# Differential attention: the next product in its last units, its casts spread over two engines, and two small VectorE instructions merged or replaced

## Chip, cores and metric

The kernel runs on one core of a Trainium2 chip. The metric is the device time of one execution in microseconds (us). Before the change three runs took 2040.03, 2040.24 and 2040.45 us; the median is 2040.24.

## The reference

Two transformer blocks over 512 tokens of width 1024, all in fp32. The first block is a sliding-window attention with retention and a convolved feed-forward; the second is a half feed-forward, a token mix and another half feed-forward. The change is in the token mix, whose first part is the differential attention (8 heads, each with two components of 64 and values of 128):

```
s = einsum('bqhcd,bkhcd->bhcqk', qb, k) * scale          # c: the two components
s = where(kpos <= qpos, s, NEG_INF)
p = softmax(s, axis=-1)
a = p[:, :, 0] - lam * p[:, :, 1]
o = einsum('bhqk,bkhe->bqhe', a, v)
y_da = rmsnorm(o, head_gain) * (1 - lam_init)
```

Behind it come the second attention (NSA: compressed, selected and windowed parts with gates), two projections, and the output product. The columns of `w_in` that give the second attention's values and gate logits are the product that the change moves.

## The kernel before

Every fp32 product is made of three passes over operands split in a high part (a cast to fp32r) and a low part (the difference): high x high, high x low, low x high (`three`, L666). Weights are streamed: chunks of 128 x 1024 are loaded by SyncE into six slots (L475 to L478), ScalarE casts the high part (`split`, L1255) and VectorE makes the low part (`split`, L1768). A chunk's slot is free when TensorE has counted it used (`w_used`). Each engine has its own program, in order; the engines meet only in semaphores.

A **unit** t of the differential attention is one head t//4 and one block t%4 of 128 query rows, so its width is 128, 256, 384 or 512 keys; there are 32. The parts of a unit are spread over the engines, two units ahead of each other:

- TensorE, step t (L853): values of unit t-2 (`values`, L825), scores of unit t+2 for both components in two PSUM banks (`scores`, L801), transpose of unit t (`turn`, L816), and one eighth of a chunk of the product `nsf` (`nsf_steps`).
- ScalarE, step t (L1450): output of unit t-2 (`da_out`), cast of the transposed probabilities (`high`), sometimes casts of the operands of a later head (`high_parts`), then the exponentials of unit t+2 (`exps`), which need the row maxima.
- VectorE, step t (L1994): `combine` (L1970: a reciprocal, the factor `gg` as a SCALAR_TENSOR_TENSOR of one element per partition, and the difference of the two components in place), `low` (the low part of the transposed probabilities), `maxima` of unit t+2 (L1963, one reduction for each component), and at the units of `LOW_AT` the low part of a weight chunk.
- GpSimd: the low parts of a head's queries and keys (`qk_low`, L537) and values (`v_low`, L553), each instruction behind a drain.

A head's operands are staged so: ScalarE casts Q and K for both components in four casts in a row (`high_parts(..., 0)`, L1467) at units with t%4 == 3 (for the head after the next), and V in one cast at t%4 == 1 (for the next head); GpSimd makes the low parts as they come (semaphore `st_hi`, counted in `st_lo`); SyncE copies the K cast to the other half of the partitions (`TWIN_AT`, L452). Scores of a head wait for `st_lo` and `k_twin` (L805), values for the fifth count of the head (L829).

Behind the attention TensorE makes the product `nst` (L1035): three chunks, four tiles each of 128 rows x 304 columns in banks 0 to 3, nine products a tile in the first two chunks and six in the last. ScalarE and VectorE meanwhile norm the attention's output: squares (L1626), their sums (L2211), a root (L1629), the multiplication by its reciprocal (L2219), then the rotated keys (`keys_out`, L2225), and the high and low parts of the product (L1635, L2239). Then `rope_q` and the compression follow (L1104).

Of the kernel before, what the change touches and what calls it, by code (L numbers as in the profile page):

```python
# [14 lines left out]
P = 128  # L15
# [8 lines left out]
LEAD = 5  # L24
# [75 lines left out]
def program(nc, t, out, stop=None):  # L100
# [9 lines left out]
    with ExitStack() as ctx:  # L110
# [170 lines left out]
        ps = [ctx.enter_context(nc.psum_tensor(f"ps{b}", [P, 512], F32)) for b in range(8)]  # L281
# [44 lines left out]
        k_twin = sem("k_twin")  # L326
        mx_done = sem("mx_done")
# [51 lines left out]
        LOW_AT = (6, 10, 14, 22, 30)  # L379
# [45 lines left out]
        def _(sp):  # L425
# [14 lines left out]
            def swaps(m):  # L440
# [51 lines left out]
        def _(pl):  # L492
# [43 lines left out]
            if on("da"):  # L536
                def qk_low(it, head):  # L537

                    u = head % 2
                    q = qkd[:, span(it, 2, head, 1), :].rearrange("p a n -> p (a n)")  # L540
                    for m in range(2):
                        own, other = slice(HD * m, HD * m + HD), slice(HD * (1 - m), HD * (1 - m) + HD)
                        pool.drain()
                        pl.wait_ge(st_hi, 5 * head + m + 1)
                        pool.tensor_tensor(Qst[other, u, m, :], q[own, :], Qst[own, u, m, :], ALU.subtract).then_inc(st_lo, 1)
                    k = qkd[:, span(it, 2, 8 + head, 1), :].rearrange("p a n -> p (a n)")
                    for m in range(2):
                        own = slice(HD * m, HD * m + HD)
                        pool.drain()
                        pl.wait_ge(st_hi, 5 * head + m + 3)  # L550
                        pool.tensor_tensor(Kl[own, u, m, :], k[own, :], Kh[own, u, m, :], ALU.subtract).then_inc(st_lo, 1)

                def v_low(it, head):  # L553
                    u = head % 2
                    pool.drain()
                    pl.wait_ge(st_hi, 5 * head + 5)
# [103 lines left out]
        def _(pe):  # L660
# [140 lines left out]
            def scores(t):  # L801
# [3 lines left out]
                if i == 0:  # L805
                    pe.wait_ge(st_lo, 5 * (t // 4) + 4)
# [18 lines left out]
            def values(t):  # L825
# [3 lines left out]
                if t % 4 == 0:  # L829
                    pe.wait_ge(st_lo, 5 * (t // 4) + 5)  # L830
# [17 lines left out]

            def attention():
# [3 lines left out]
                for t in range(TOTAL):  # L853
# [181 lines left out]
            if on("nst"):  # L1035
                for c in range(3):
                    s = weights(CHUNK0["nst"] + c)
                    for tt in range(TT):
                        q = slice(tt * P, (tt + 1) * P)
                        if c == 0:  # L1040
                            bank_free("nst", tt)
                        for j, k in enumerate(range(c * VG_K, min(c * VG_K + VG_K, KT))):
                            n = slice(j * VG_W, (j + 1) * VG_W)
                            last = three(ps[tt][:, 0:VG_W], HTh[:, k, q], HTl[:, k, q], Wh[:, s, n], Wl[:, s, n], k == 0, k == KT - 1)
                    last.then_inc(w_used, 1)
# [208 lines left out]
        def _(ac):  # L1254
# [183 lines left out]
            def nsf_out(c):  # L1438
                chunk_done("nsf", c)
                if c >= 2:  # L1440
                    ac.wait_ge(st_lo, 5 * (4, 7)[c - 2] + 2)
# [3 lines left out]
            def attention():  # L1445
                exps(0)
                high_parts(0, 0, 1)
                exps(1)
                high_parts(0, 1, 0)
                for t in range(TOTAL):  # L1450
# [16 lines left out]
            def high_parts(it, head, which):  # L1467

                u = head % 2
                if which == 0:  # L1470
                    q = qkd[:, span(it, 2, head, 1), :].rearrange("p a n -> p (a n)")
                    for m in range(2):
                        own = slice(HD * m, HD * m + HD)
                        scalar.copy(Qst[own, u, m, :], q[own, :]).then_inc(st_hi, 1)
                    k = qkd[:, span(it, 2, 8 + head, 1), :].rearrange("p a n -> p (a n)")
                    for m in range(2):
                        own = slice(HD * m, HD * m + HD)
                        scalar.copy(Kh[own, u, m, :], k[own, :]).then_inc(st_hi, 1)
                else:
                    if head == 0:  # L1480
                        ac.wait_ge(free[6], FREED["da"][6])
                    scalar.copy(Vst[:, u, 0, :].rearrange("p (t n) -> p t n", t=TT), vd[:, :, span(it, 2 * P, head * P, P)]).then_inc(st_hi, 1)
# [128 lines left out]
            if on("vda"):  # L1611
                for c in range(7):
                    split(CHUNK0["vda"] + c + LEAD)
                    if c == 3 and on("da"):
                        ac.wait_ge(roped, 24)
                        high_parts(0, 0, 0)
# [5 lines left out]
            if on("nsf"):  # L1622
# [5 lines left out]
                ac.wait_ge(da_ss, 2)  # L1628
                scalar.activation(hsd[:], hss[:], ACT.Sqrt, scale=1.0 / P, bias=eps[:]).then_inc(da_sd, 1)  # L1629
            if on("nst"):  # L1630
                split(CHUNK0["nst"] + 1 + LEAD)
# [4 lines left out]
                for tt in range(TT):  # L1636
                    scalar.activation(gates[:, tt, :], ps[tt][:, 2 * P:VG_W], ACT.Sigmoid).then_inc(vs_hi, 1)
# [944 lines left out]
```

## Time and profile before

| | us |
|---|---|
| median of 3 runs | 2040.24 |
| profiled execution, own time | 2040.7 |
| its span in the trace | 2038.9 |
| TensorE busy | 1990.8 (98%) |
| VectorE busy | 1052.6 (52%) |
| ScalarE busy | 818.6 (40%) |
| GpSimd busy | 275.5 (14%) |
| mean granted TensorE clock | 0.993 |

The profile is one execution on the chip. Times in the trace are counted from the span's start; the differential attention lies between 1107 and 1220 us. PE is TensorE's matmul queue and PEld its weight loads, DVE is VectorE, ACT is ScalarE, POOL is GpSimd, SP is SyncE. A granted clock of 1.00 is 2.4 GHz and 0.50 is 1.2 GHz. "<-" in a bracket names what ended a wait.

### The profile page before, as it was taken

The numbers are of one execution on the slowest core, as the hardware profiler recorded it, in microseconds if no ns is written. First come the engines' busy times: TensorE is split into PE (matmuls) and PEld (weight loads), VectorE is DVE, ScalarE is ACT, GpSimd is POOL, SyncE is SP. The second block draws the span as 40 slices with busy tenths as digits, with TensorE's granted clock in tenths as the row PEclk, the third lists the DMA queues.
The fourth block names the chain that finished last, engine by engine and source line by source line (L and its number), as shares of the span: only waits on it lengthen the run. The fifth ranks groups of instructions, "written<-read, shape, count | busy, mean of one in ns | idle before, by whom it ended". The sixth has DMA issues, their size and how long they took to land.

```text
span 2038.9 us, 25594 instructions
## 1 busy us (share of the span) xinstructions
PE 1990.8 (98%) x10180; PEld 1681.7 (82%) x10180; DVE 1052.6 (52%) x1607; ACT 818.6 (40%) x1489; POOL 275.5 (14%) x275
## 2 busy tenths in 40 slices
PE   6999999999999999999999889999999999999998
PEld 6888888888889888888987679788888888888887
DVE  5675665555353222333654768877764542222333
ACT  5442543333343222233334774466664332222332
POOL 1000000000000000000003534287861000000000
PEclk9999999999999999999999989999999999999999
DMA  5331333233323333332443125311216423333332
GB/s 197 99 99 52 114 104 103 94 94 103 93 93 95 103 93 95 102 93 73 150 140 104 32 91 183 93 47 48 63 48 206 120 82 104 99 98 93 103 94 73
DMA packets 60262, 202.23 MB, mean 99 GB/s; under 512 B 8336, under 2 KB 8368, under 8 KB 59760
## 3 DMA queue, kind: packets, MB, share of 16 engines
q1 hardware_dynamic: 55936, 184.58, 29.5%
q0 software_dynamic: 4208, 16.01, 2.3%
q8 instruction: 82, 1.34, 0.3%
q14 instruction: 36, 0.29, 0.0%
HBM read 181.16 MB, written 8.39 MB: 93 GB/s over the span
## 4 chain that ended last, share of the span: by engine, by line
PE 90%; DVE 4%; ACT 3%; DMA 1%; DVEq 1%; issue 1%; SPq 0%; ACTq 0%
PE ps L667 26%; PE ps L669 26%; PE ps L668 26%; PE ps L1141 2%; PE ps L1130 1%; DMA raw<-in_w_all 1%; PE ps L1131 1%; PE ps L1179 1%; PE ps L1178 1%; DVE XN L1814 1%; PE ps L1057 1%; ACT XN L1294 1%; DVE nmx L1968 1%; DVE HTl L1823 0%; PE ps L1132 0%
## 5 line engine op out<-in xcount | busy, mean ns | idle before, releaser
L1774 DVE TENSOR_TENSOR Wl<-raw,Wh 128x1024 fp32r<-128x1024 f32 x307 | 380.7, 1242 | 692.7 <-ACT Wh L1261 691.1
L667 PE MATMUL ps<-HTh,Wh 128*128 128x512 f32 (+1 forms) x1728 | 649.7, 376 | 8.7 <-DVE HTl L1823 6.9
L669 PE MATMUL ps<-HTh,Wl 128*128 128x512 f32 (+1 forms) x1728 | 642.2, 372 | 0.0
L668 PE MATMUL ps<-HTl,Wh 128*128 128x512 f32 (+1 forms) x1728 | 642.0, 372 | 0.0
L1261 ACT CAST Wh<-raw 128x1024 fp32r<-128x1024 f32 x307 | 322.0, 1052 | 739.8 <-DMA raw<-in_w_all 739.7
L667 PEld LDWEIGHTS ps<-HTh,Wh 128*128 128x128 f32 x1728 | 327.6, 190 | 63.2 <-issue 9.7
L669 PEld LDWEIGHTS ps<-HTh,Wl 128*128 128x128 f32 x1728 | 327.1, 189 | 56.5
L668 PEld LDWEIGHTS ps<-HTl,Wh 128*128 128x128 f32 x1728 | 327.5, 190 | 52.8
L667 PE MATMUL ps<-Wh,Yh 128*128 128x512 f32 x528 | 205.8, 390 | 0.0
L669 PE MATMUL ps<-Wh,Yl 128*128 128x512 f32 x528 | 205.5, 389 | 0.0
L668 PE MATMUL ps<-Wl,Yh 128*128 128x512 f32 x528 | 205.4, 389 | 0.0
L623 POOL TENSOR_SCALAR PU<-PU,ugg 128x512 f32<-128x512 f32 (+3 forms) x128 | 139.2, 1103 | 79.3 <-DVE ugg L2349 79.3
L667 PE MATMUL ps<-Wh,HTh 128*128 128x512 f32 (+2 forms) x320 | 119.8, 374 | 0.0
L669 PE MATMUL ps<-Wh,HTl 128*128 128x512 f32 (+2 forms) x320 | 118.8, 371 | 0.0
L668 PE MATMUL ps<-Wl,HTh 128*128 128x512 f32 (+2 forms) x320 | 118.7, 371 | 0.0
L668 PEld LDWEIGHTS ps<-Wl,Yh 128*128 128x128 f32 x528 | 99.1, 188 | 20.6
L669 PEld LDWEIGHTS ps<-Wh,Yl 128*128 128x128 f32 x528 | 99.1, 188 | 20.5
L667 PEld LDWEIGHTS ps<-Wh,Yh 128*128 128x128 f32 x528 | 99.1, 188 | 20.4
L1693 ACT ACTIVATE PU<-ps,umx 128x512 f32<-128x512 f32 (+3 forms) x128 | 65.7, 525 | 53.4 <-DVE umx L2341 53.4
L669 PEld LDWEIGHTS ps<-Wh,HTl 128*128 128x128 f32 x320 | 60.8, 190 | 10.0
L668 PEld LDWEIGHTS ps<-Wl,HTh 128*128 128x128 f32 x320 | 60.9, 190 | 9.8
L667 PEld LDWEIGHTS ps<-Wh,HTh 128*128 128x128 f32 x320 | 61.0, 190 | 9.7
(279 smaller groups left out, 2327.1 us busy)
## 6 DMA issues: line engine op xcount, KB each, us to landing
raw<-in_w_all SPq DMA_DIRECT2D x307, 512.0 KB, 3.5
swp_d<-qkd SPq DMA_DIRECT2D x64, 64.0 KB, 2.8
g_dram<-gst SPq DMA_DIRECT2D x16, 256.0 KB, 3.9
ring<-g_dram POOLq DMA_DIRECT2D x16, 256.0 KB, 3.7
gpre<-in_g_pre POOLq DMA_DIRECT2D x5, 512.0 KB, 4.9
X<-in_x SPq DMA_DIRECT2D x4, 512.0 KB, 4.9
swp_r<-qkr SPq DMA_DIRECT2D x16, 128.0 KB, 3.7
Kh<-Kh SPq DMA_DIRECT2D x16, 128.0 KB, 2.3
```

The costliest lines, as they stand in the source:

```text
L623: last = pool.tensor_scalar(p, p, ugg[:, s % 2, i:i + 1], None, ALU.mult)
L667: tensor.matmul(dst, a_hi, b_hi, start=start, stop=False)
L668: tensor.matmul(dst, a_hi, b_lo, start=False, stop=False)
L669: return tensor.matmul(dst, a_lo, b_hi, start=False, stop=stop)
L1057: last = tensor.matmul(ps[kv][:, ht * 64:ht * 64 + 62], cw[:, j, ht * P:(ht + 1) * P], cA[:, kv, j, :], start=j == 0, stop=j == 15)
L1130: tensor.matmul(ps[b][:, o:o + w], q, ksh[:, m, g, 0:w], start=True, stop=False)
L1131: tensor.matmul(ps[b][:, o:o + w], q, ksl[:, m, g, 0:w], start=False, stop=False)
L1141: return tensor.transpose(dst, p[:, a:a + P], ident[:])
L1178: tensor.matmul(ps[b][:, k * P:], v, AUh[:, o:o + w], start=False, stop=False)
L1261: scalar.copy(Wh[:, s, :], raw[:, s, :]).then_inc(w_hi, 1)
L1693: last = scalar.activation(PU[:, (s + 1) % 2, SCORE_AT[i]:SCORE_AT[i] + w], ps[b][:, o:o + w], ACT.Exp, bias=umx[:, s % 2, i:i + 1], accum ...
L1774: vector.tensor_tensor(Wl[:, s, :], raw[:, s, :], Wh[:, s, :], ALU.subtract).then_inc(w_lo, 1)
```

## The change

It does these things:

- The tiles of the first two chunks of `nst` become a function, `nst_tile`, and are issued in the attention's last units: two tiles behind each of the steps 29, 30 and 31, and two between the value products of units 30 and 31. Only the third chunk stays behind the attention.
- The K casts leave ScalarE for GpSimd, at the head of `qk_low`, which now waits (from head 2 on) for the cast of unit 4(head-2)+2; a new semaphore `k_hi` tells SyncE of them. GpSimd's order per head becomes K casts, K low parts, Q low parts, and then the V low part of the head before.
- ScalarE's Q casts are split over the ends of the units with t%4 == 2 and 3, and the V cast goes to the end of the head's own unit with t%4 == 0; all of them now stand behind `exps`.
- The factor `gg` becomes a TENSOR_SCALAR with two per-partition scalars.
- The row maxima of both components become one reduction over two PSUM banks, which are now one tensor.
- Behind the attention ScalarE takes the product's casts and sigmoids before the root, and VectorE the product's low parts before the multiplication by the reciprocal root. The last low part of a weight chunk goes from unit 30 to 31.

```diff
-        ps = [ctx.enter_context(nc.psum_tensor(f"ps{b}", [P, 512], F32)) for b in range(8)]
+        banks = ctx.enter_context(nc.psum_tensor("ps", [P, 8, 512], F32))
+        ps = [banks[:, b, :] for b in range(8)]
...
-        LOW_AT = (6, 10, 14, 22, 30)
+        LOW_AT = (6, 10, 14, 22, 31)
...
-                        sp.wait_ge(st_hi, 5 * head + 4)
+                        sp.wait_ge(k_hi, 2 * head + 2)
...
                 def qk_low(it, head):
+                    k = qkd[:, span(it, 2, 8 + head, 1), :].rearrange("p a n -> p (a n)")
+                    if head >= 2:
+                        pl.wait_ge(at_hi, 4 * (head - 2) + 3)
+                    for m in range(2):
+                        own = slice(HD * m, HD * m + HD)
+                        pool.drain()
+                        pool.tensor_copy(Kh[own, u, m, :], k[own, :])
+                        pool.drain().then_inc(k_hi, 1)
+                    for m in range(2):
+                        own = slice(HD * m, HD * m + HD)
+                        pool.drain()
+                        pool.tensor_tensor(Kl[own, u, m, :], k[own, :], Kh[own, u, m, :], ALU.subtract).then_inc(st_lo, 1)
...
-                for it in range(3):
-                    for head in (1, 2):
-                        v_low(0, 2 * it + head)
-                        qk_low(0, 2 * it + head + 1)
+                for head in range(2, 8):
+                    qk_low(0, head)
+                    v_low(0, head - 1)
...
+            def nst_tile(c, tt):
+                s = weights(CHUNK0["nst"] + c)
+                q = slice(tt * P, (tt + 1) * P)
+                if c == 0:
+                    bank_free("nst", tt)
+                for j, k in enumerate(range(c * VG_K, min(c * VG_K + VG_K, KT))):
+                    n = slice(j * VG_W, (j + 1) * VG_W)
+                    last = three(ps[tt][:, 0:VG_W], HTh[:, k, q], HTl[:, k, q], Wh[:, s, n], Wl[:, s, n], k == 0, k == KT - 1)
+                if tt == TT - 1:
+                    last.then_inc(w_used, 1)
...
+                    if t == TOTAL - 3:
+                        nst_tile(0, 0)
+                        nst_tile(0, 1)
+                    if t == TOTAL - 2:
+                        nst_tile(0, 2)
+                        nst_tile(0, 3)
+                    if t == TOTAL - 1:
+                        nst_tile(1, 0)
+                        nst_tile(1, 1)
                 values(TOTAL - 2)
+                nst_tile(1, 2)
+                nst_tile(1, 3)
                 values(TOTAL - 1)
...
-                    if t % 4 == 1 and exists(t + 4):
-                        high_parts(0, t // 4 + 1, 1)
-                    if t % 4 == 3 and exists(t + 5):
-                        high_parts(0, t // 4 + 2, 0)
+                    head = t // 4 + 2
                     if exists(t + 2):
                         exps(t + 2)
+                    if t % 4 == 2 and head < 8:
+                        q_high(head, 0)
+                    if t % 4 == 3 and head < 8:
+                        q_high(head, 1)
+                    if t % 4 == 0 and t:
+                        v_high(t // 4)
...
-                    vector.tensor_reduce(nmx[:, u, m:m + 1], ps[2 * u + m][:, 0:w], AX.X, ALU.max, negate=True).then_inc(mx_done, 1)
+                vector.tensor_reduce(nmx[:, u, :], banks[:, 2 * u:2 * u + 2, 0:w], AX.X, ALU.max, negate=True).then_inc(mx_done, 2)
...
-                vector.scalar_tensor_tensor(out=gg[:, v, 0:1], in0=rs[:, u, 0:1], scalar=nlam[:], in1=rr[:, t % STEPS, 1:2],
-                                            op0=ALU.mult, op1=ALU.mult)
+                vector.tensor_scalar(gg[:, v, 0:1], rs[:, u, 0:1], nlam[:], rr[:, t % STEPS, 1:2], ALU.mult, ALU.mult)
```

## Rows read from the trace of the kernel before

**Rows 1.** Busy time by stretch: stretch, us, PE, PEld, DVE, ACT, POOL, clock, DMA share, GB/s.
```profile
1159.00:1172.00 13.00, 11.12 (x77) 8.97 (x76) 10.57 (x26) 9.68 (x30) 7.09 (x5) 1.00 0.10 22
1199.00:1214.00 15.00, 10.57 (x80) 8.74 (x78) 12.74 (x31) 10.98 (x34) 2.37 (x3) 0.97 0.65 214
1214.00:1222.00 8.00, 7.34 (x32) 7.16 (x33) 1.30 (x3) 2.43 (x4) 1.07 (x2) 0.50 0.02 2
1222.00:1251.00 29.00, 29.00 (x161) 26.26 (x160) 27.69 (x31) 15.17 (x25) 18.85 (x18) 0.98 0.58 199
```

**Rows 2.** Waits from 1107 to 1216 us: in total, times, longest.
```profile
PEld ps L822 <- DVE Pb L1981: 12.6, 15, 1.6
```

**Rows 3.** The chain of waits, one head: start, us, engine, line.
```profile
1139.41 0.62 ACT Qst L1474
```

**Rows 4.** Timeline of ScalarE, units 2 and 26: start us, us, instruction.
```profile
1121.14 0.48 ACT L1431 CAST ATdh<-ps 128x384 fp32r<-128x384 f32 x1 [1.09 <-PE ps L822]
...
1202.03 0.48 ACT L1431 CAST ATdh<-ps 128x384 fp32r<-128x384 f32 x1 [1.08 <-PE ps L822]
```

**Rows 5.** Groups by line and shape, 1107 to 1216 us: busy, mean ns, idle before.
```profile
L551 POOL TENSOR_TENSOR Kl<-qkd,Kh 64x512 fp32r<-64x512 f32 x14 | 19.8, 1417 | 2.2 <-issue 2.2
L545 POOL TENSOR_TENSOR Qst<-qkd,Qst 64x512 fp32r<-64x512 f32 x14 | 17.9, 1279 | 29.3 <-ACT Qst L1474 28.2 <-issue 1.0 <-ACT Kh L1478 0.2
L558 POOL TENSOR_TENSOR Vst<-vd,Vst 128x512 fp32r<-128x512 f32 x8 | 12.3, 1541 | 27.5 <-ACT Vst L1482 27.5
L1978 DVE SCALAR_TENSOR_TENSOR gg<-rs,nlam,rr 128x1 f32<-128x1 f32 x32 | 13.6, 426 | 3.1 <-issue 0.9
...
L1981 DVE SCALAR_TENSOR_TENSOR Pb<-Pb,gg 128x512 f32<-128x512 f32 x8 | 6.0, 751 | 0.6
...
L1968 DVE TENSOR_REDUCE nmx<-ps 128x1 f32<-128x512 f32 x16 | 10.3, 685 | 3.1 <-PE ps L814 3.1
```

**Rows 6.** One line's instructions, a later stage: duration ns least/median/most.
```profile
L613 POOL CAST QSn<-qnr x16: 602/606/613, 1272.0 to 1499.5; 64x512 fp32r<-64x512 f32 x16
```

**Rows 7.** Timeline, a head's first value product and third unit's cast.
```profile
1159.26 0.22 PE L667 MATMUL ps<-Vst,ATdh 128*128 128x128 f32 x1
...
1161.13 0.49 ACT L1431 CAST ATdh<-ps 128x384 fp32r<-128x384 f32 x1
```

**Rows 8.** Timeline of VectorE and GpSimd around one factor.
```profile
1155.43 1.26 POOL L551 TENSOR_TENSOR Kl<-qkd,Kh 64x512 fp32r<-64x512 f32 x1 [0.16 <-issue]
...
1155.79 0.92 DVE L1978 SCALAR_TENSOR_TENSOR gg<-rs,nlam,rr 128x1 f32<-128x1 f32 x1
```

**Rows 9.** Timeline at the attention's start.
```profile
1110.83 1.29 POOL L558 TENSOR_TENSOR Vst<-vd,Vst 128x512 fp32r<-128x512 f32 x1 [19.24 <-ACT Vst L1482]
...
1120.56 0.55 PE L822 MATMUL ps<-ident,Pb 128*128 128x128 f32 x3 [1.48 <-DVE Pb L1981]
```

**Rows 10.** One line's instructions: a TENSOR_SCALAR of one element.
```profile
L2058 DVE TENSOR_SCALAR nlam<-nlam x1: 155/155/155, 64.1 to 64.1; 128x1 f32<-128x1 f32 x1
```

**Rows 11.** Timeline of TensorE, the attention's end and the product behind it.
```profile
1206.99 0.31 PE L667 MATMUL ps<-Vst,ATdh 128*128 128x128 f32 x1
...
1208.36 0.45 PE L812 MATMUL ps<-Kh,Qst 128*128 128x512 f32 x1
...
1209.52 0.39 PE L822 MATMUL ps<-ident,Pb 128*128 128x128 f32 x2
...
1220.21 0.56 PE L667 MATMUL ps<-Wh,HTh 128*128 128x304 f32 x1
...
1231.78 0.31 PE L667 MATMUL ps<-Wh,HTh 128*128 128x304 f32 x1
...
1234.98 0.30 PE L669 MATMUL ps<-Wh,HTl 128*128 128x304 f32 x1
```

**Rows 12.** Timeline: VectorE's long pause and TensorE's next wait.
```profile
1272.27 0.48 DVE L2254 MEMSET hid<- 128x512 f32 x1 [7.16 <-ACT hid L1642]
...
1320.01 1.38 PE L1141 MATMUL ps<-ident,PU 128*128 128x128 f32 x10 [1.06 <-DVE CAl L2305]
```

More of the change, by code:

```diff
@@ L378, in program, with qk_parts, v_parts, q_parts @@
         HIGH_AT = (2, 6, 10, 18, 26)
-        LOW_AT = (6, 10, 14, 22, 30)
+        LOW_AT = (6, 10, 14, 22, 31)
+        def qk_parts(head):
+            return (0, 5)[head] if head < 2 else 5 * head - 1
+        def v_parts(head):
+            return min(9 + 5 * head, 40) if head else 5
+        def q_parts(head):
+            return (0, 3)[head] if head < 2 else 3 * head - 1
+        def v_casts(head):
+            return min(5 + 3 * head, 24) if head else 3
         def nsf_ends(t):
@@ L543, in qk_low @@
                         pool.drain()
-                        pl.wait_ge(st_hi, 5 * head + m + 1)
+                        pl.wait_ge(st_hi, q_parts(head) + m + 1)
                         pool.tensor_tensor(Qst[other, u, m, :], q[own, :], Qst[own, u, m, :], ALU.subtract).then_inc(st_lo, 1)
[L546 to L551, printed above, removed]
                 def v_low(it, head):
@@ L555, in v_low @@
                     pool.drain()
-                    pl.wait_ge(st_hi, 5 * head + 5)
+                    pl.wait_ge(st_hi, v_casts(head))
                     by_tile = lambda a: a.rearrange("p (t n) -> p t n", t=TT)
@@ L1035, in _ @@
             if on("nst"):
[L1036 to L1045, printed above, removed]
+                for tt in range(TT):
+                    nst_tile(2, tt)
             if on("cmp"):
@@ L1446, in attention @@
                 exps(0)
[L1447 removed]
+                v_high(0)
                 exps(1)
[L1449 removed]
+                qk_high(1)
                 for t in range(TOTAL):
@@ L1465, in attention, with q_high, qk_high, v_high @@
                 da_out(TOTAL - 1)
-            def high_parts(it, head, which):
+            def q_high(head, m):
                 u = head % 2
[L1470 to L1482, printed above, removed]
+                own = slice(HD * m, HD * m + HD)
+                scalar.copy(Qst[own, u, m, :], qkd[own, head, :]).then_inc(st_hi, 1)
+            def qk_high(head):
+                q_high(head, 0)
+                q_high(head, 1)
+            def v_high(head):
+                u = head % 2
+                if head == 0:
+                    ac.wait_ge(free[6], FREED["da"][6])
+                scalar.copy(Vst[:, u, 0, :].rearrange("p (t n) -> p t n", t=TT), vd[:, :, head * P:head * P + P]).then_inc(st_hi, 1)
             ac.wait_ge(boot, 1)
@@ L1637, in _ @@
                     scalar.activation(gates[:, tt, :], ps[tt][:, 2 * P:VG_W], ACT.Sigmoid).then_inc(vs_hi, 1)
+            if on("nsf"):
+                ac.wait_ge(da_ss, 2)
+                scalar.activation(hsd[:], hss[:], ACT.Sqrt, scale=1.0 / P, bias=eps[:]).then_inc(da_sd, 1)
+            if on("nst"):
+                split(CHUNK0["nst"] + 1 + LEAD)
                 split(CHUNK0["nst"] + 2 + LEAD)
@@ L2215, in _ @@
                 split(CHUNK0["nst"] + LEAD)
+            if on("nst"):
+                for tt in range(TT):
+                    ve.wait_ge(vs_hi, tt + 1)
+                    for m in range(2):
+                        last = vector.tensor_tensor(vhl[m][:, tt, :, HD:P], ps[tt][:, m * P:(m + 1) * P].rearrange("p (g d) -> p g d", g=2),
+                                                    vhl[m][:, tt, :, 0:HD], ALU.subtract)
+                    last.then_inc(free[tt], 1)
+            if on("nsf"):
                 ve.wait_ge(da_sd, 1)
@@ L2238, in _ @@
             if on("nst"):
-                for tt in range(TT):
-                    ve.wait_ge(vs_hi, tt + 1)
-                    for m in range(2):
-                        last = vector.tensor_tensor(vhl[m][:, tt, :, HD:P], ps[tt][:, m * P:(m + 1) * P].rearrange("p (g d) -> p g d", g=2),
-                                                    vhl[m][:, tt, :, 0:HD], ALU.subtract)
-                    last.then_inc(free[tt], 1)
                 keys_out(1)
```

12 lines of the change are left out of this document (5 added, 7 removed).

## The prediction

> **What bounds the kernel now.** I read the page's share by engine first: TensorE is busy nearly all the span, so only places where it stands or runs at its lower clock can give time. The busy times by stretch find them: in the differential attention a head of four units takes 13 us of which TensorE is busy 11.1, and from 1199 to 1214 us it is busy 10.6 of 15; then from 1214 to 1222 it works at a granted clock of 0.50, the 1.2 GHz level [rows 1]. The list of waits names what ends last there: above all the transposes of TensorE wait for VectorE's combination of the two components [rows 2]. The chain of waits shows what is late before it: once per head ScalarE casts query and key parts in a row, and the exponentials stand behind them in its queue [rows 3]. How slow the stage is: the cast of unit 2's transposed probabilities starts at 1121.14 us, that of unit 26 at 1202.03, so six heads take 80.89 us, 13.48 each [rows 4].
>
> **The change part by part.** (a) *Casts spread and moved.* ScalarE's four casts in a row (0.62 us each) become one at the end of unit 2, one at the end of unit 3 and the V cast in unit 0; the two key casts go to GpSimd. ScalarE is relieved of 1.24 us a head and no exponential waits behind more than one cast. GpSimd takes them at 0.61 us each, by a cast of the same shape later in the kernel [rows 6].
>
> What is late next? GpSimd now has a fixed chain per head: it starts when unit 4h+2 is cast by ScalarE (the new wait), then two key casts, two K differences, two Q differences and the V difference of the head that comes next, each behind a drain. Queued behind each wait on GpSimd is all the rest, and the V difference is awaited by TensorE's value product of unit 4h+4. Its length: 2 x 0.61 + 4 x 1.28 + 1.27 = 7.61 us [rows 5, 6], plus seven gaps of 0.16 us, 8.73 us. The loop closes over TensorE: from the value product of the head's first unit to the end of ScalarE's cast of its third, in the kernel before 1159.26 to 1161.62 us, 2.36 us [rows 7]. With two semaphore hops, estimated at 0.1 us each, 11.3 us.
>
> Then come the holds. VectorE's one-element factor takes 0.92 us where it is free to run in 0.22; it ends at 1156.71, where GpSimd's difference, begun at 1155.43, ends at 1156.69. The two engines exclude each other in these instructions [rows 8], and the hold goes both ways: GpSimd's K differences take 1.42 us on average where its Q differences, of the same shape, take 1.28, and the V difference 1.54 where the least seen is 1.29 [rows 5, 9]. So GpSimd loses 2 x 0.14 + 0.25 = 0.5 us per head in five operations; for seven, and with VectorE met more often, I take 0.9. The loop is then 12.2 us a head. Bounds: below, TensorE's own 11.1 busy in such a head [rows 1]; above, each of the seven operations held for a whole combination, for which I estimate 0.55 us as the mean over widths from the 0.75 us of the widest [rows 5], 15.0. I take 12.25: the loop is short of nothing but its own work, and the nearest rows are its own operations. Six heads: 80.9 - 73.5 = 7.4 us less.
>
> At the start, head 1's parts come later: from the V difference at 1110.83 us, 1.29 + 7.3 + some hold gives 1119.9, when before the transposes of unit 2, held by GpSimd too, started at 1120.56 [rows 9]. I charge nothing; if the scores of unit 4 stand on it fully, it costs 2 us.
>
> (b) *Factor from one operand.* 0.22 us becomes about 0.155, the time of a TENSOR_SCALAR of one element [rows 10]; with VectorE not the bound it counts nothing by itself. The factor no longer has two tensor inputs, so I expect it not to be held; but the combination right behind it has two and is held until the same moment. What is saved is the factor and its drain, 0.23 us, where a hold falls. That is cover inside the 12.25, worth 0 to 4 us over the stage.
>
> The Trainium skill speaks against this step: SBUF — State Buffer, section "Who interferes with whom", says that `tensor_scalar` can enter a two-port mode and then contends with GpSimd. No row before shows such an instruction beside GpSimd's work. By that rule the factor is held as before, and the edit gives nothing but the 0.065 us.
>
> (c) *One maximum over two banks.* One start of an instruction is saved; I estimate a tenth of the 0.685 us of the widest, 0.07 us a unit. Against it, the instruction starts only when both banks are full, and VectorE already waits for scores before the widest reductions, 3.1 us over 16 [rows 5]; the first reduction then no longer lies beside the second component's scores, and the first exponential waits for both. I take 0, since the loop of (a) does not run over VectorE. Bounds: 32 x 0.07 = 2.2 us gained, or one widest reduction in each of eight heads, 5.5 us, lost.
>
> (d) *The next product among the last units.* Eight tiles of nine products move from behind the attention into its end. In the kernel before, the transpose of unit 29 starts at 1209.52, and the product that follows the attention at 1220.21, with waits and half clock between [rows 1, 11]; its last of 24 starts at 1234.98, so 25.5 us to its end. After: value products of units 28 to 31, ten blocks at 0.34 us (four took 1206.99 to 1208.36), 3.4; two transposes 0.8; 72 products of 304 columns at 0.139 us (23 steps from 1231.78 to 1234.98), 10.0; the last chunk's 24, 3.3: 17.5 us [rows 11]. With no half clock, since TensorE doesn't stand. That is 8.0 less, and 7.6 with 0.4 for waits that stay. Bounds: 3 us if the clock falls all the same and a wait stays, 8.
>
> Then VectorE's cover is gone: its sums of squares, norms and key rotation ran beside that product, busy 27.7 of 29 us [rows 1], and the attention's end itself comes 3.8 us later after unit 29. But its next long pause is 7.16 us, before 1272.27; after it TensorE waits only 1.06 us at 1320.01 [rows 12]. Counting pauses of some 12 us between the attention's end and 1320 against the 11.4 us that TensorE arrives sooner after that end, VectorE is just level. I charge 1.5 us; bounds 0 and 6. The reordering of sigmoid and root on ScalarE, and the later low cast (unit 31 for 30), move work between these pauses and cost nothing apart: the chunk concerned is wanted 15 us later.
>
> Sum: 7.4 + 7.6 - 1.5 = 13.5 us. The profiled execution took 2040.7 us, 1.8 around its span; so 2027.2, and the median lies 0.46 lower: 2026.8 us.
>
> **The rivals.**
> 1. *TensorE becomes the bound* (the holds stay small). For: ScalarE and VectorE have 2 us a head free. Against: the GpSimd loop alone is 11.3. 6 x (13.48 - 11.1) = 14.3, + 7.6 - 1.5: 2019.8.
> 2. *The factor is held as before*, so VectorE's chain, with more GpSimd work to meet, keeps 0.23 us in three of four units of six heads, 4.1 us: 2030.9. For: any small instruction before the combination was held; against: the reciprocal, one tensor input, was not.
> 3. *The casts were not what ended last*: the burst is replaced by holds and the head stays at 13.48. For: the longest waits name the combination; against: chain and burst. Gain 6.1: 2034.1.
> 4. *VectorE gives the end's gain back*: 6 us instead of 1.5: 2031.3; with the clock falling as well, 2036.
> 5. *Slower: GpSimd's chain.* One mechanism: each operation held a full combination, each combination a full operation. At 15.0 us a head, 6 x 1.52 = 9.1 lost, 6.1 gained: 2043.2. It decides from 14.5 us a head on. Against: it needs over four times the holding per head seen now.
> 6. *No gain*: the moved product meets chunks not yet split and waits where it stands, head at 13.48. Its chunks are split by unit 14, so this is weak: 2040.
>
> **Numbers.** Forecast 0.42; rival 1 0.13, 2 0.13, 3 0.12, 4 0.10, 5 0.05, 6 0.05. A measurement here can tell 0.2%, 4.1 us, from no change. Rival 5 is the slower side; rival 6 and a quarter of rival 3 lie inside that bound; the rest is faster: faster 0.87, same 0.08, slower 0.05. Range: 2019 (rival 1) to 2036 (rivals 3 and 4).
>
> **What would show it.** The casts of units 2 and 26 (width 384) should lie some 73.5 us apart. GpSimd should be busy over 9 us of each 12, its V difference ending just before TensorE's value product of a head's first unit, and TensorE's wait there put down to GpSimd. The factor should take 0.16 us at most in all 32, and the combination show the hold. No granted clock below 1 after 1209 us, with TensorE busy all through the last three units. The product's last part should end some 17.5 us after the transpose of unit 29. VectorE's 7 us pause should be gone, with TensorE waiting 1 to 3 us near the first units of the next attention. The prediction is wrong if the head stays above 13 us, if it goes under 11.5, or if TensorE stands for more than 4 us behind the product.

## The result and the profile after

The changed kernel takes 2047.62 us (median of 9 runs), the kernel before on the same chip 2040.24: ratio 1.0032, interval 1.0023 to 1.0040. It is slower, by 7.4 us or 0.3%, where 13.5 us less were forecast. The profiled execution took 2047.76 us with a span of 2045.8. Its page's first rows, and the granted clock in 40 slices:

```profile
PE 1998.7 (98%) x10180; PEld 1690.7 (83%) x10180; DVE 1045.4 (51%) x1575; ACT 810.1 (40%) x1473; POOL 286.9 (14%) x291
...
PEclk9999999999999999999999997999999999999999
```

TensorE is busy 8 us longer with the same work, and one slice (1227 to 1278 us) has a lower clock. The busy times by stretch, columns as in [rows 1], say where (the clock is the third column from the end):

```profile
1199.00:1214.00 15.00, 14.51 (x111) 13.22 (x111) 10.77 (x23) 10.03 (x30) 2.40 (x3) 1.00 0.52 150
1214.00:1222.00 8.00, 8.00 (x64) 8.00 (x63) 0.69 (x1) 1.55 (x4) 0.91 (x2) 1.00 0.59 233
...
1250.00:1260.00 10.00, 3.78 (x18) 2.78 (x17) 9.37 (x11) 5.39 (x6) 0.00 (x0) 0.80 0.74 252
1260.00:1270.00 10.00, 9.55 (x45) 9.55 (x45) 3.85 (x5) 1.36 (x3) 0.00 (x0) 0.50 0.48 142
1270.00:1280.00 10.00, 10.00 (x49) 10.00 (x48) 2.69 (x4) 1.56 (x2) 3.73 (x4) 0.50 0.01 2
1280.00:1290.00 10.00, 10.00 (x41) 8.33 (x41) 8.09 (x13) 2.57 (x3) 0.00 (x0) 0.84 0.12 22
```

The end of the attention is what was forecast: TensorE is busy 14.5 of 15 us where it was 10.6, and the half clock from 1214 to 1222 us is gone [rows 1]. Thirty us later, where the kernel before had TensorE at work without a break at clock 1.00, TensorE stands 6 of 10 us and then works at 0.50, the 1.2 GHz level. TensorE's timeline (start us, us, instruction, idle before and what ended it):

```profile
1240.36 7.25 PE L1094 MATMUL ps<-cA,cw1k 128*128 128x62 f32 x64
...
1255.10 0.63 PE L1102 MATMUL ps<-hid,w2k 128*128 128x62 f32 x4 [1.95 <-ACT hid L1684]
1260.45 13.92 PE L1094 MATMUL ps<-cA,cw1v 128*128 128x62 f32 x64 [4.71 <-DMA cw1v<-in_cw]
1274.16 7.04 PE L1124 MATMUL ps<-kcb,qn 128*128 128x64 f32 x32
1280.95 0.77 PE L690 MATMUL ps<-HTh,Wh 128*128 128x512 f32 x1
```

In the kernel before the same instructions run

```profile
1251.46 7.25 PE L1057 MATMUL ps<-cA,cw1k 128*128 128x62 f32 x64
...
1264.48 7.31 PE L1057 MATMUL ps<-cA,cw1v 128*128 128x62 f32 x64
1271.62 3.74 PE L1087 MATMUL ps<-kcb,qn 128*128 128x64 f32 x32
1275.17 0.48 PE L667 MATMUL ps<-HTh,Wh 128*128 128x512 f32 x1
```

TensorE reaches the first compression product 11.1 us sooner and rope_q's chunk 4 (L690, L667) 5.8 us later. Who is late is read from the queues. ScalarE of the changed kernel:

```profile
1242.58 1.05 ACT L1298 CAST Wh<-raw 128x1024 fp32r<-128x1024 f32 x1 [6.87 <-DMA raw<-in_w_all]
1250.03 1.91 ACT L1714 CAST ksh<-ksw 128x2048 fp32r<-128x2048 f32 x1 [6.41 <-DVEq L2289]
1251.85 0.59 ACT L1697 ACTIVATE qn<-ps 128x512 f32<-128x512 f32 x1
1252.33 1.04 ACT L1298 CAST Wh<-raw 128x1024 fp32r<-128x1024 f32 x1
1253.39 1.28 ACT L1684 ACT_TABLE_LOAD   x1
1254.69 0.27 ACT L1684 ACTIVATE hid<-ps 128x124 f32<-128x124 f32 x1
```

The product for `hid` ends at 1247.6, but its activation stands behind a cast that waits for VectorE's `ks_f`, behind a query and behind a weight cast. SyncE issues its DMAs in order as well:

```profile
1232.42 4.82 SPq L484 DMA_DIRECT2D y_dram<-YD  x4
1237.30 0.51 SPq L495 DMA_DIRECT2D raw<-in_w_all  x1
1241.92 3.38 SPq L456 DMA_DIRECT2D qnr<-qn  x4
1245.35 0.58 SPq L495 DMA_DIRECT2D raw<-in_w_all  x1
1249.97 2.41 SPq L456 DMA_DIRECT2D qnr<-qn  x4
1252.42 0.59 SPq L487 DMA_DIRECT2D cw1v<-in_cw  x1
```

The 2 MB of `cw1v` are issued behind the swap of chunk 1, which waits for VectorE's `roped` (kept back by its second key rotation, to 1249.9); they take 8.0 us to land. VectorE's chain hangs on the attention's end. Counted from the attention's first score product, ScalarE's last output of the attention came only 2.0 us sooner than before (111.1 for 113.1 us) and VectorE's second key rotation ended only 1.7 sooner, while TensorE reached the compression 13.5 us sooner; TensorE alone had run ahead.

**One ledger for all kernels.** F is the first score product of the attention, H the first product of the compression, R rope_q's chunk 4, T the first transposes of the next attention ([rows 12] has before's). us, from each profiled execution:

```
kernel                   units 2-26   F to H   H to R   R to T   median us
before                      80.89     144.12    23.71    44.84   2040.24
changed                     74.29     130.67    40.59    46.06   2047.62
e1 load early               74.73     130.63    39.15    46.94   2046.02
e2 no product               74.14     138.77    33.98    46.44   2046.68
e3 product alone            78.31     136.42    38.46    46.00   2043.28
e8 filled                   74.55     130.67    31.42    44.83   2037.90
e4 load and cast            74.20     130.68    39.30    46.16   2044.94
e5 e4, factor undone        75.35     131.16    38.89    46.76   2045.08
e6 e4, maxima undone        70.87     126.23    39.38    47.22   2041.65
e9 before, e4's moves       78.32     140.58    23.71    44.85   2040.30
e10 queues, b, c undone     72.59     128.43    23.71    47.82   2028.93
e11 queues alone            74.42     130.67    23.71    47.90   2033.43
e12 e10, no product         72.58     131.44    23.71    44.86   2031.65
e13 queues, c undone        70.84     126.20    23.71    47.08   2025.91
```

Behind T the two traces have the same 718.8 and 718.9 us left. F itself lies between 1106.6 and 1110.2 us from one execution to another (before 1107.34, changed 1109.69), work that no kernel here touches; so spans differ by up to 3.6 us for nothing, and F to H leaves that out. F to H has a scatter of its own, though. e9 has the attention of the kernel before unchanged, and takes 140.58 us where the trace before has 144.12. The mean granted clock in the trace before is 0.83 from 1117 to 1127 us, 0.91 from 1167 to 1187 and 0.91 from 1222 to 1230; in e9's it is 1.00 in all three. So a difference of F to H between two traces can be off by 3.5 us where their clocks differ. H to R is 23.71 us wherever TensorE has no wait in it. The changed kernel has 16.9 more: from the `cw1v` product to R 20.50 us against 10.69, so 9.8 for the clock, and 7.1 for standing. The half clock lasts some 2 us beyond R, and R to T is 1.2 us longer too. Together F to T is 4.65 us longer than before; the other 2.35 of the 7.0 between the two spans lie ahead of F.

### The profile page after: what moved, and what is told of

It reads as the page before. It is cut to its first block, busy times and chain, and to the rows that moved or that the text cites. A ratio compares the mean times of both kernels' runs of the same rounds, so it can differ in the third digit from the quotient of the medians.

```text
span 2045.8 us, 25629 instructions
## 1 busy us (share of the span) xinstructions
PE 1998.7 (98%) x10180; PEld 1690.7 (83%) x10180; DVE 1045.4 (51%) x1575; ACT 810.1 (40%) x1473; POOL 286.9 (14%) x291
## 4 chain that ended last, share of the span: by engine, by line
PE 65%; issue 24%; DVE 4%; ACT 2%; DMA 1%; DVEq 1%; POOLq 1%; SPq 0%; POOL 0%; ACTq 0%
PE ps L690 18%; PE ps L691 18%; PE ps L692 18%; PE ps L1178 2%; PE ps L1167 1%; DMA raw<-in_w_all 1%; PE ps L1168 1%; PE ps L1216 1%; PE ps L1215 1%; DVE XN L1856 1%; PE ps L1094 1%; DVEq L2019 1%; ACT XN L1331 1%; PE ps L1124 1%; PE ps L1169 0%
## 5 line engine op out<-in xcount | busy, mean ns | idle before, releaser
L690 PE MATMUL ps<-HTh,Wh 128*128 128x512 f32 (+1 forms) x1728 | 650.7, 377 | 8.7 <-DVE HTl L1865 6.9
L690 PEld LDWEIGHTS ps<-HTh,Wh 128*128 128x128 f32 x1728 | 328.4, 190 | 63.6 <-issue 9.8
L690 PE MATMUL ps<-Wh,Yh 128*128 128x512 f32 x528 | 205.8, 390 | 0.0
L690 PE MATMUL ps<-Wh,HTh 128*128 128x512 f32 (+2 forms) x320 | 120.0, 375 | 0.0
L690 PEld LDWEIGHTS ps<-Wh,Yh 128*128 128x128 f32 x528 | 99.1, 188 | 20.4
L692 PEld LDWEIGHTS ps<-Wh,HTl 128*128 128x128 f32 x320 | 60.4, 189 | 10.3
L690 PEld LDWEIGHTS ps<-Wh,HTh 128*128 128x128 f32 x320 | 60.5, 189 | 9.8
```

The lines of the kernel that those rows point to most:

```text
L690: tensor.matmul(dst, a_hi, b_hi, start=start, stop=False)
L692: return tensor.matmul(dst, a_lo, b_hi, start=False, stop=stop)
```

## The experiments

**e1: the load of cw1v early.** Right behind the y_dram copies, issued at 1239.97.

```
 if m == CHUNK0["nst"] + 2 ...:      # behind the four y_dram copies
+    sp.wait_ge(yd_out, 16 * TT)
+    sp.dma_start(cw1v ...)
-if m == CHUNK0["rope_q"] + 1 ...: the same two lines
```

> The changed kernel, with one edit on SyncE: the 2 MB load of cw1v stands right behind the copy of the attention's output to DRAM, ahead of the swaps of the first two rope_q chunks. Theory A (the loss is TensorE's wait for this load, which stands in SyncE's queue behind the swap that waits for the second keys_out, and the half clock that follows): the load is issued near 1240 us instead of 1252.4 and lands before TensorE asks for it; the 4.7 us wait goes, and with it most of the stretch at 0.50; TensorE reaches rope_q's fifth chunk about 15 us sooner than in the changed kernel. 2047.6 minus 12 to 17: 2031 to 2036. Theory B (VectorE's own queue is the bound behind the attention, and the wait for the load only covers it): TensorE waits for VectorE or ScalarE instead at the same place, 2044 to 2048. Theory C (the loss lies in the attention, where GpSimd holds VectorE more): no change, 2047.

2046.02 us, ratio 1.0026 (1.0015 to 1.0037). That is theory B's time, with ScalarE as the one that is late. The load's wait is gone, and another has taken its place: TensorE waits for `hid`, ScalarE having stood 16.46 us for `raw` (6.87 in the changed kernel). That load is now issued at 1240.35 for 1237.30, since SyncE first waits 3.6 us for the y_dram copies to land, and it lies behind the 2 MB.

```profile
1257.21 1.08 PE L1101 MATMUL ps<-hid,w2k 128*128 128x62 f32 x4 [5.03 <-ACT hid L1683]
```

One wait of the two was late behind the other; mending one gives nothing.

**e2: the next product whole behind the attention**, the rest of the change kept.

```
-    if t == TOTAL - 3: nst_tile(0, 0); nst_tile(0, 1)      # and so on
+for c in range(3):
+    for tt in range(TT):
+        nst_tile(c, tt)
```

> The changed kernel with the product nst whole behind the attention again; casts, factor and maxima stay as changed, and so does the new order of ScalarE and VectorE behind the attention. Theory A: the attention keeps its 12.4 us a head and the product covers the load as before: 2040.2 minus 5 to 7, plus 1 for the start: 2034 to 2037. Theory C: the attention part costs time: 2041 to 2048.

2046.68 us, 1.0033 (1.0021 to 1.0045). So the kernel is slower without the moved product too. The time is theory C's, but its reason isn't: the attention takes less time than before. H comes 138.8 us behind F, 5.4 sooner than before, and that is already too soon:

```profile
1260.46 12.34 PE L1084 MATMUL ps<-cA,cw1v 128*128 128x62 f32 x64 [1.88 <-DMA cw1v<-in_cw]
```

A stand of 1.88 us, the clock at 0.50 behind it, and H to R is 10.3 us over its 23.71: 8.4 besides the stand.

**e3: the kernel before with TensorE's product moved, nothing else.**

```
+    if t == TOTAL - 3:
+        nst_tile(0, 0)
+        nst_tile(0, 1)
...
```

> The kernel before with only TensorE's tiles of nst moved into the attention's last units; casts, factor, maxima and the order behind the attention as before. Theory A: the attention's end gains 7 to 8 us on TensorE, and the wait for cw1v and the half clock take it back and more, as in the changed kernel: 2046 to 2053 (the changed kernel plus the attention's 6.5 us, less what a later TensorE waits less: the stall is tied to the attention's end in both). Theory C: 2032 to 2035.

2043.28 us, 1.0030 (1.0015 to 1.0045); seven of its twelve executions took 2039 to 2043 us and five 2050 to 2054. The profiled one is of the upper group, inside theory A's range; the median lies outside both theories, and no trace shows the lower group. F to H falls by 7.7 us, but 2.6 of them lie between the casts of units 2 and 26, where this kernel is the one before: its trace has no half clock there, as e9's. From unit 26's cast to H it takes 44.3 us, where the kernel before takes 49.4 and e9 48.5. H to R rises by 14.7: `cw1v` is late by 4.33 us and the clock falls. The order behind the attention is the old one here, so the reordering isn't needed for the stand.

**e8: idle products in the place of the stand.** The changed kernel with 34 products of 512 columns into bank 5, which nothing reads there, ahead of the compressed keys.

```
+for n in range(34):
+    tensor.matmul(ps[5][:], HTh[:, 0, 0:P], HTh[:, 1, :], start=True, stop=True)
 cmp_keys()
 cmp_hidden(1)
```

> The changed kernel with 34 products of 512 columns more on TensorE, into an unused bank, between rope_q's fourth chunk and the compression's keys: 34 x 0.226 = 7.7 us, as long as TensorE stands there (2.0 and 4.7 us and the short work between). Nothing reads them. It tells the wait from the clock: if the granted clock stays at 1.00, the stretch of 27 us at 0.50 gives back 10 to 13 us while the wait stays filled: theory A, 2035 to 2039. If the clock isn't what costs (the engines that follow would be late anyway), the time stays at 2046 to 2048 or rises by what isn't covered.

2037.9 us, 0.9986 (0.9977 to 0.9995): 9.7 us under the changed kernel, by work that computes nothing. The rows of TensorE:

```profile
1250.70 7.87 PE L1147 MATMUL ps<-HTh 128*128 128x512 f32 x34
1258.41 0.55 PE L1102 MATMUL ps<-hid,w2k 128*128 128x62 f32 x4
1258.80 7.31 PE L1094 MATMUL ps<-cA,cw1v 128*128 128x62 f32 x64
```

H to R is 31.42: 7.7 us of filling stay, the 9.8 of the clock are gone. That separates the two prices, and shows that the clock falls here because TensorE stands: the granted clock is 1.00 from 1240 to 1280 us.

**e4, e5, e6, e9: both moves, parts undone.** e4 is e1 with the cast of ksh behind hidden(0) on ScalarE; e5 is e4 with the factor as before (b), e6 is e4 with the two maxima as before (c), e9 is the kernel before with e4's two moves.

```
 if c == 2:
     hidden(0)
+    ac.wait_ge(cm_a, 2)      # these three lines stood at c == 1
+    ac.wait_ge(ks_f, 1)
+    scalar.copy(ksh ...)
```

> The changed kernel with the cw1v load early, as in e1, and ScalarE's cast of the rotated keys (ksh) behind the first compression's activation instead of ahead of the third query copy, so that it no longer keeps that activation from TensorE. In e1 TensorE waited 5.0 us for that activation and the clock fell as in the changed kernel; with both edits nothing before the second compression product should wait. Theory A (loss = waits there and the half clock behind them): granted clock 1.00 from 1250 to 1290 us, the product with cw1v starting near 1252; 2028 to 2033. Theory B (VectorE's queue is the bound): TensorE waits later, at the scores or the fifth rope_q chunk, and the clock falls there: 2040 to 2046.

2044.94 us, 1.0019 (1.0010 to 1.0028). The time is theory B's, but TensorE doesn't wait where that theory had it. `hid` is still 5.18 us late: on ScalarE it stands behind weight casts for chunks 4 and 5, which aren't wanted yet, and their loads lie behind the 2 MB.

```profile
1250.51 1.05 ACT L1297 CAST Wh<-raw 128x1024 fp32r<-128x1024 f32 x1 [16.99 <-DMA raw<-in_w_all]
```

> e4 with the factor as a SCALAR_TENSOR_TENSOR again (two tensor inputs). In the changed kernel the new form took 0.273 us in all 32, against 0.22 unheld before, and was never held. If being held matters: 1 to 4 us above e4. If only the 0.05 us counts: equal to e4 or up to 1 us below.

2045.08 us, 1.0022 (1.0013 to 1.0031). The time is the same. The six heads take 1.15 us more; from F to H only 0.5 is left of it, for e4's trace has more half clock near unit 2 (0.66 on average from 1117 to 1127 us, e5's 0.83). The factor's edit is a small gain, not a loss; 1 to 4 us are not seen here.

> e4 with one reduction for each component again. In the changed kernel ScalarE waits 11.3 us in all for the merged maximum, 16 times, and VectorE 18.9 us for scores (11.7 before). If these waits are on the path: 2 to 6 us below e4. If the head is set by GpSimd's chain: equal to e4 within 1 us.

2041.65 us, 1.0004 (0.9996 to 1.0013). Two maxima make the six heads 3.3 us shorter and F to H 4.5. So the merged maximum costs 4.5 us here. What is late with it and not without it stands in the waits of e4 and then e6, 1107 to 1216 us (in total, times, longest):

```profile
ACT Pb L1458 <- DVE nmx L2008: 11.3, 16, 0.8
ACT ATdh L1467 <- PE ps L844: 11.2, 20, 1.9
```

```profile
ACT ATdh L1467 <- PE ps L844: 17.1, 26, 1.6
```

ScalarE's first exponential waits for the maximum 16 times in e4, and e6's list has no such wait, though it waits longer for the transposes; in all ScalarE waits 5.4 us less for the two. VectorE's own reductions take nearly the same, 1.22 us for 1024 columns against twice 0.68 for 512, but the merged one starts only when the second bank is full.

> The kernel before with the two edits of e4 (load early, ksh cast late), nothing of the change. There TensorE had no wait behind the product, so nothing is to be gained: 2039 to 2041. If it is faster, part of e4's gain doesn't belong to the change.

2040.3 us, 0.9995 (0.9986 to 1.0004), and 23.71 us from H to R as without the moves. Where TensorE arrives late enough, the order of the queues costs nothing.

**e10, e11, e12: the queues mended at the places that the last traces name.** The load of cw1v goes behind the next weights and ahead of the swap of chunk 0, and ScalarE takes query(2) and hidden(0) ahead of the weight cast of chunk 4.

```
 c = m - CHUNK0["rope_q"]
+if c == 0 and on("cmp"):
+    sp.wait_ge(yd_out, 16 * TT)
+    sp.dma_start(cw1v ...)
...
-    query(c)
+    if c != 2: query(c)
+    if c == 1: query(2); hidden(0)
     split(CHUNK0["rope_q"] + c + LEAD)
+    if c == 2: (the cast of ksh and its waits)
```

e11 is the changed kernel with this alone; e10 also has the factor and the maxima as before; e12 is e10 with the product whole behind the attention.

> The changed kernel with the factor and the two maxima as before, cw1v's load issued behind the y_dram copies and ahead of the swap of rope_q's chunk 0, and on ScalarE query(2) and hidden(0) ahead of the cast of chunk 4 (so no instruction that hidden(0) stands behind waits for a load or for ks_f). Theory (what cost the change its gain are two in-order queues, and then the half clock that the standing brings): hidden(0) ends near 1241, the activation comes within 2 us, cw1v has landed by 1246, TensorE stands under 1 us between 1240 and 1265, granted clock 1.00 throughout 1240 to 1300; the time 2032 us (2029 to 2036). Rival (VectorE is the bound from here on, and the time lost in standing only hides its lateness): TensorE stands for the low half of chunk 4 instead, as long as before, and the time is 2038 to 2042. Second rival (the 2 MB load ahead of the swap holds the swap and the weights of chunk 5 back): a wait of over 4 us for raw on ScalarE in front of rope_q(4) or (5), 2037 to 2041.

2028.93 us, 0.9943 (0.9930 to 0.9955). No wait between H and R; ScalarE takes `hid` as soon as TensorE has it:

```profile
1243.52 0.27 ACT L1684 ACTIVATE hid<-ps 128x124 f32<-128x124 f32 x1 [5.19 <-PE ps L1094]
```

The first rival is out. It comes back in small: behind R, TensorE waits 2.27 us for VectorE's copy of the gates (`gst`), and the granted clock is 0.50 from 1299 to 1302 us. The second rival's wait is there, 5.4 us for `raw` on ScalarE, but TensorE never waits for it.

> The changed kernel with the two moves in the queues alone (cw1v's load ahead of the swap of chunk 0; query(2) and hidden(0) ahead of the cast of chunk 4), factor from one operand and one maximum over two banks kept. Theory: the product ends near 1253 as in the changed kernel, TensorE stands under 1 us behind it, clock 1.00, and the time is that of the kernel filled with idle products or a little under it: 2037 us (2034 to 2040). If VectorE is the bound: 2042 to 2046. The difference to the first kernel of this group is what the two small edits cost: 4 us if the cost of the merged maxima stays on the path as it did at the end of attention (last cast of ATdh at 1206.9 us with two, 1211.3 with one).

2033.43 us, 0.9959 (0.9946 to 0.9972). Two moves in two queues turn the slower kernel into a faster one: it is 14.2 us under the changed kernel, of which the traces show 16.9 won between H and R and 1.8 lost behind R. Neither move was tried without the other at these places. I had expected 2037, since I took the filled kernel for the measure; the filling itself was on the path.

> The first kernel of this group with the next product whole behind the attention, as in the kernel before: spread casts and the two mended queues are all that is left of the change. Theory of my sum: the product's move is worth the 8 us only as far as VectorE's chain behind it lets TensorE use them; with the queues mended TensorE arrives about 10 us later than in the first kernel and stands nowhere: 2034 us if the path is VectorE's from rope_q(4) on (then 0 to 2 us slower than the first), 2040 if TensorE's work bounds this stretch (8 us slower than the first).

2031.65 us, 0.9958 (0.9944 to 0.9972). Without the moved product H comes 3.0 us later than in e10, not 8, for in e12 the clock stays at 1.00 at the attention's end anyway, as e2's did not (first row e2, second e12):

```profile
1210.00:1215.00 5.00, 4.54 (x21) 4.36 (x21) 0.19 (x1) 1.32 (x3) 0.77 (x2) 0.50 0.64 272
```

```profile
1210.00:1215.00 5.00, 5.00 (x37) 5.00 (x37) 3.03 (x2) 4.66 (x3) 1.48 (x3) 1.00 0.51 198
```

And T lies at the same distance from F in both (200.01 and 199.96 us): e10 hands the 3.0 us back behind R, by a wait for VectorE of 2.27 us where e12 has 0.87, and by the half clock behind it. VectorE is later there for a reason: the moved tiles stand ahead of unit 31's value product, so ScalarE's last output of the attention comes 108.9 us behind F in e10 and 101.8 in e12. The two spans are equal; whether the 2.7 us between the medians are more than scatter isn't settled.

**e13: the best of the parts.** The changed kernel with the mended queues and two maxima.

```
-vector.tensor_reduce(nmx[:, u, :], banks[:, 2 * u:2 * u + 2, 0:w], ..., negate=True).then_inc(mx_done, 2)
+    vector.tensor_reduce(nmx[:, u, m:m + 1], ps[2 * u + m][:, 0:w], ..., negate=True).then_inc(mx_done, 1)
```

> The changed kernel with the two moves in the queues (cw1v's load ahead of the swap of chunk 0; query(2) and hidden(0) ahead of the cast of chunk 4) and the two maxima as before; casts spread, factor from one operand and the product among the last units kept. Theory from the stretch between unit 2's and unit 26's cast, 74.20 us with everything, 75.35 without the factor, 70.87 without the merged maxima, 72.59 without both: the factor from one operand saves 1.2 to 1.7 us there, the merged maxima cost 2.8 to 3.3. So here 70.9 us (70.4 to 71.5), hidden(0) starts 126.2 us after the first score, TensorE does not stand for hid or cw1v, clock 1.00 from 1230 to 1290. Whether that reaches the end: if TensorE bounds the stretch behind, 2027 us, some 1.7 under the kernel with the old factor (2028.93); if VectorE's chain behind the attention bounds it, the same 2029 (2027.5 to 2030.5). Rival: TensorE, arriving 2 us sooner, stands for hid or cw1v again, the clock falls to 0.50, and the time is over 2034.

2025.91 us, 0.9936 (0.9923 to 0.9950), 21.7 us under the changed kernel (13.3 under the kernel before on its own chip) and the fastest here. The times of the stretches came as expected. The six heads take 70.84 us, 11.8 each; F to H 126.20. The first wait behind H is VectorE's:

```profile
1297.44 0.47 PE L690 MATMUL ps<-HTh,Wh 128*128 128x512 f32 x1 [3.09 <-DVE gst L2413]
```

This wait is longer than e10's at the same place, and yet the granted clock stays at 1.00 from 1290 to 1310 us.

## Why the prediction was wrong

**The step that failed** is the one behind the product: "VectorE is just level. I charge 1.5 us; bounds 0 and 6." It cost 16.9 us between H and R. I had compared TensorE's lead with the sum of VectorE's pauses up to 1320 us. But TensorE doesn't wait for a sum; it waits at its next two meeting points, `hid` and `cw1v`, and neither is made by VectorE: one lies in ScalarE's queue behind a wait for VectorE, the other in SyncE's behind another. The trace before had what was needed:

```profile
1251.79 0.58 SPq L469 DMA_DIRECT2D cw1v<-in_cw  x1
...
DMA to landing us min/median/max: 9.2/9.2/9.2
...
1258.74 0.27 ACT L1642 ACTIVATE hid<-ps 128x124 f32<-128x124 f32 x1 [4.26 <-PE ps L1057]
```

`cw1v` landed at 1261.0 and was wanted at 1264.48, and ScalarE had stood ready for `hid` for 4.26 us. The leads that these two could bear were 3.5 and 4.3 us, and I was forecasting one of 15. e1 and e4 show that SyncE's queue alone, or with the cast of ksh, wasn't enough; e11 shows that with both queues mended nothing is left of the cost between H and R.

**The size of it** comes from the clock. I had 5 us at most for "the clock falling as well" (rival 4, 2036 us). The stands, 7.1 us, cost 9.8 us besides their own length up to R and 1.2 behind it, the most expensive part of the whole result (e8 is the kernel without that cost). My line for being wrong, TensorE standing over 4 us behind the product, was met, and none of my rivals held its price; the one that ended slower was looked for in the attention, where the change was, and not behind it.

**(a) and (c): a right sum of two wrong terms.** The six heads take 74.29 us, 12.38 each, for a forecast of 12.25. The loop of (a) is there. In the changed kernel's trace GpSimd's V difference ends at 1159.31, TensorE's value product starts 0.09 us later, and GpSimd's next casts start at 1161.68, 12.11 us behind those of the head before (1149.57). TensorE's short wait ahead of the value product is put down to "issue", not to GpSimd as I had expected:

```profile
1158.03 1.28 POOL L582 TENSOR_TENSOR Vst<-vd,Vst 128x512 fp32r<-128x512 f32 x1 [0.16 <-issue]
1159.40 0.30 PE L690 MATMUL ps<-Vst,ATdh 128*128 128x128 f32 x1 [0.56 <-issue]
1161.68 0.99 POOL L564 CAST Kh<-qkd 64x512 fp32r<-64x512 f32 x1 [2.38 <-ACT ATdh L1468]
```

But e13 and e11 differ only in the maxima, 70.84 to 74.42: the casts with the new factor bring a head to 11.8 us (the casts with the old factor, e10, to 12.1), and (c), taken as 0, costs 3.6 us there and 4.5 up to H. It was the lower bound (5.5 us lost) that was nearer, by the reason given beside it: the reduction waits for both banks, and the first exponential for both. I set it to 0 because the loop of (a) didn't run over VectorE. It does by its last leg: GpSimd's wait for ScalarE's cast is 2.39 us in e11 and 2.22 in e13 in the heads around 1150 us, and its Q differences take 1.36 us on average against 1.28; such a head takes 12.1 us in e11 and 11.7 in e13. The rest of the 3.6 us is in the later heads, in part by the clock: e11's mean granted clock is 0.84 from 1167 to 1177 us, e13's 1.00. Of the kernels with spread casts, the seven with the merged maximum all have a mean granted clock of 0.96 from 1107 to 1187 us, the four without all have 0.98; whether the merging brings it on wasn't tested by itself. GpSimd's holds came in the casts, not the differences:

```profile
L575 POOL TENSOR_TENSOR Qst<-qkd,Qst 64x512 fp32r<-64x512 f32 x14 | 19.0, 1360 | 2.6 <-issue 2.4 <-ACT Qst L1511 0.2
L569 POOL TENSOR_TENSOR Kl<-qkd,Kh 64x512 fp32r<-64x512 f32 x14 | 17.9, 1282 | 2.8 <-issue 2.8
...
L564 POOL CAST Kh<-qkd 64x512 fp32r<-64x512 f32 x14 | 12.2, 875 | 17.4 <-ACT ATdh L1468 15.6 <-issue 1.6
```

The casts, 0.61 us apiece in [rows 6], take 0.88 on average: four lie beside no VectorE instruction and take 0.60 or 0.61, and the ten others, 0.77 to 1.03, lie beside one with two tensor inputs. Together the holds come to 2 x 0.27 + 2 x 0.08 = 0.7 us a head, for 0.9 taken; the size was near, the place was not. (My upper bound for a head adds up to 15.15, not 15.0.) The start, charged nothing with 2 us as its price, is 1.0 longer, 14.83 us from F to unit 2's cast against 13.80; but with two maxima (e6, e13) it is 13.79 and 13.80. So the moved casts cost nothing there, and this is a part of what (c) costs.

**(b)** The factor takes 0.273 us in all 32, not 0.155, and is never held:

```profile
L2020 DVE TENSOR_SCALAR gg<-rs,nlam,rr x32: 272/273/274, 1112.9 to 1209.7; 128x1 f32<-128x1 f32 x32
```

With the factor of before it is 0.545 us on average in e10. The edit saves 1.2 us of six heads in e5 and 1.7 in e10 against e13. The rule of the Trainium skill that I weighed against it (SBUF — State Buffer, "Who interferes with whom", by which a `tensor_scalar` can enter a two-port mode, under conditions on its operands, and then contends with GpSimd) didn't bite here, and my "By that rule the factor is held" left the conditions out: 20 of these 32 lie beside a computing instruction of GpSimd, 14 of them wholly, and all 32 agree within 2 ns.

**(d)** was right: from the transpose of unit 29 to the product's last instruction 17.54 us (1206.34 to 1223.88), for 17.5 forecast and 25.46 before. From e2 to the changed kernel F to H falls by 8.1, for 7.6 to 8.0 forecast. Most of it, however, was the half clock that it happened to avoid: where the clock stays up without it, it is worth 3.0 us up to H and nothing at T (e12, e10).

So the forecast's 15.0 us up to H came as 13.5 between these two traces (9.9 against e9's); what the prediction got wrong is what happens to a lead once it is won.

## What to carry to other kernels

When an edit makes an engine arrive sooner by some us, list its next few meeting points in order and write beside each when the other side is ready now; the smallest slack, not the sum of pauses, is the lead that can be used, and in-order queues (DMA issues too) are followed back through what stands ahead. Put no instruction that waits for something late, or prepares something wanted later, ahead of one that the bounding engine needs next. And price a stand of TensorE with the clock that may follow it: here the clock cost more than the stand.

## What the runs showed of the hardware

- In e6 TensorE stood 5.26 us before 1251.75; the granted clock fell during that stand and was 0.50 (1.2 GHz) until 1278 us, though TensorE worked without a break from 1251.75 on. The work was products of 62 and 64 columns up to 1273.1, and of 512 behind. After a stand of 1.88 us (e2) it was at 0.50 too, `cw1v` taking 12.34 us for 7.31. Products into an unread bank kept the clock at 1.00 (e8).
- Not every stand does it: behind R one of 2.27 us was followed by 3 us at 0.50 (e10, from 1299), one of 3.09 us by none (e13).
- A TENSOR_SCALAR of one element with two per-partition operands took 0.273 us, one with a constant 0.155 [rows 10]. The former was not held beside GpSimd (20 times of 32), where the scalar-tensor-tensor form, 0.22 us free, was, up to 1.28 us in the trace before.
- Casts of GpSimd are held as well: 0.61 us free, 1.03 at most.
- One maximum over two banks costs what two do, less about a tenth: 1.223 us for 1024 columns, 0.685 for 512.
